# The memory norm of a fused two-block kernel: its sum of squares and its inverse root on other engines

## The reference, cut to what matters

```
def rmsnorm(x, g):
    xf = x.astype(jnp.float32)
    r = lax.rsqrt(jnp.mean(xf * xf, axis=-1, keepdims=True) + EPS)
    return (xf * r * g.astype(jnp.float32)).astype(x.dtype)

# in second_block, after the mixing part and the attention:
h = h + merged @ w_out[l]
c = rmsnorm(h, g_cross[l])
m = rmsnorm(mem, g_mem[l])            # mem: 256 positions x 1024
h = h + memory_cross_attention(c, m, w_q_cross[l], w_kv_cross[l], w_o_cross[l])
```

## Time and profile before

| | us |
|---|---|
| median of 3 runs | 2732.92 (2732.54 to 2734.36) |
| the profiled execution's own time | 2734.61 |
| its span, first to last instruction | 2732.6 |
| TensorE busy | 2679.1 (98%) |
| GpSimd busy | 1566.7 (57%) |
| VectorE busy | 1761.8 (64%) |
| ScalarE busy | 1120.9 (41%) |
| mean granted TensorE clock, of full speed | 0.995 |

### The profile page before, as it was taken

How to read it: one execution, slowest core, us unless ns; L and a number is a source line. 1 busy time by engine, 2 the same in 40 slices (tenths; PEclk the granted TensorE clock), 3 DMA queues, 4 the chain that set the end, 5 groups by cost and what they waited for, 6 DMA issues and landing times.

```text
span 2732.6 us, 37392 instructions
## 1 busy us (share of the span) xinstructions
PE 2679.1 (98%) x13692; PEld 2171.9 (79%) x13692; DVE 1761.8 (64%) x2628; ACT 1120.9 (41%) x2186; POOL 1566.7 (57%) x1175
## 2 busy tenths in 40 slices
PE   7999999999999999999999999999999999999998
PEld 6777788778888888878877777888788788888886
DVE  6776755587776777771133557763478777777776
ACT  5644422343444444454443335211354444444444
POOL 3233243567887778657722223456525787777884
PEclk9999999999999999999999999999999999999999
DMA  3110102111121221133211110342201211221112
GB/s 137 32 32 32 44 17 93 51 55 61 55 62 60 64 62 54 51 135 116 82 39 39 32 33 32 116 177 70 62 23 40 66 59 58 62 66 55 61 52 81
DMA packets 110702, 171.96 MB, mean 63 GB/s; under 512 B 7872, under 2 KB 61632, under 8 KB 108480
## 3 DMA queue, kind: packets, MB, share of 16 engines
q1 hardware_dynamic: 100352, 133.20, 15.4%
q10 hardware_dynamic: 10176, 36.44, 3.6%
HBM read 153.88 MB, written 15.73 MB: 62 GB/s over the span
## 4 chain that ended last, share of the span: by engine, by line
PE 90%; DVE 3%; POOL 3%; issue 2%; ACT 1%; DMA 1%; SPq 0%; ACTq 0%; DVEq 0%; POOLq 0%
PE PS L1485 13%; PE PS L1486 13%; PE PS L1487 13%; PE PS L1141 10%; PE PS L1143 9%; PE PS L1142 9%; PE PS L1757 2%; PE PS L1759 2%; PE PS L1758 2%; PE PS L1259 1%; PE PS L1177 1%; PE PS L1180 1%; PE PS L1178 1%; PE PS L1248 1%; PE PS L1630 1%
## 5 line engine op out<-in xcount | busy, mean ns | idle before, releaser
L907 POOL TENSOR_TENSOR WH<-WRAW,CST 128x512 fp32r<-128x512 f32 x164 | 185.4, 1131 | 709.4 <-PE PS L1143 618.3
L1141 PE MATMUL PS<-XH,WH 128*128 128x512 f32 x960 | 400.8, 418 | 2.6 <-POOL WL L909 1.7
L3374 DVE TENSOR_TENSOR H<-H,PS 128x512 f32<-128x512 f32 x560 | 367.4, 682 | 42.2 <-PE PS L1487 42.1
L1143 PE MATMUL PS<-XH,WL 128*128 128x512 f32 x960 | 377.2, 393 | 0.0
L1142 PE MATMUL PS<-XL,WH 128*128 128x512 f32 x960 | 376.5, 392 | 0.0
L942 POOL TENSOR_TENSOR WL<-WRAW,WH 128x512 fp32r<-128x512 f32 x174 | 252.3, 1451 | 118.4 <-ACT WH L2266 89.0
L942 POOL TENSOR_TENSOR WL<-XX,WH 128x512 fp32r<-128x512 f32 x148 | 202.1, 1367 | 91.4 <-ACT WH L2266 90.8
L1485 PE MATMUL PS<-XH,WH 128*128 128x512 f32 x640 | 249.4, 390 | 1.3 <-POOL WL L942 1.2
L1487 PE MATMUL PS<-XH,WL 128*128 128x512 f32 x640 | 249.0, 389 | 0.0
L1486 PE MATMUL PS<-XL,WH 128*128 128x512 f32 x640 | 249.0, 389 | 0.0
L1486 PE MATMUL PS<-PL,WH 128*128 128x512 f32 x624 | 242.8, 389 | 0.0
(11 more groups left out here) (443 smaller groups left out, 6104.8 us busy)
## 6 DMA issues: line engine op xcount, KB each, us to landing
WRAW<-ws SPq DMA_DIRECT2D x84, 512.0 KB, 3.5
WRAW<-ws SPq DMA_DIRECT2D x148, 256.0 KB, 2.6
XX<-ws SPq DMA_DIRECT2D x108, 256.0 KB, 2.7
RAWX<-ws SPq DMA_DIRECT2D x68, 256.0 KB, 2.6
gate_spill<-TG ACTq DMA_DIRECT2D x28, 256.0 KB, 2.1
H<-xT ACTq DMA_DIRECT2D x4, 1024.0 KB, 10.9
H<-xT ACTq DMA_DIRECT2D x2, 2048.0 KB, 10.9
h_spill<-H ACTq DMA_DIRECT2D x1, 4096.0 KB, 13.1
```

Of the source, the lines that this page charges most:

```text
L907: pool.tensor_tensor(WH[:, j, c], WRAW[:, j, c], ONES[:, 0:1].to_broadcast((P, 512)), ALU.mult).then_inc(hi_split, 1)
L1141: pe.matmul(out, WH[:, j, w], rh(kt), start=(n == 0), stop=False)
L1143: last = pe.matmul(out, WL[:, j, w], rh(kt), start=False, stop=(n == len(kts) - 1))
L3374: dve.tensor_tensor(x, x, PS[:, 4 + t], ALU.add).then_inc(h_added, 1)
```

## The change

The sum of squares is first folded on VectorE: three additions in XX, 128x1024, 128x512 and 128x256, halve the eight channel tiles to one. TensorE then makes one product of a 128x128 matrix of ones with that 128x256 tile, so the sum over channels arrives on every partition, and the 16 products and the two spreading products go. ScalarE divides by 1024, adds epsilon and writes 128x256 from PSUM to RAWX (Identity where the square root was). VectorE writes -0.5 into a column of STAT where the reciprocal was. GpSimd raises the 128x256 tile to that power into the other half of RAWX; for this, its loop over units is cut in two behind unit 63. VectorE's 8 multiplications read RAWX in SBUF where they read PSUM.

The diff, without the renamed semaphores:

```diff
--- before.py
+++ after.py
@@ -1110,7 +1110,13 @@
-            with pool.Fori(i + 1, U_FFN2 // 2) as i:
+            with pool.Fori(i + 1, U_WO2 // 2 + 2) as i:
+                for j in range(2):
+                    split_unit(i, j, True)
+            pool.wait_ge(mem_root, 1)
+            pool.wait_ge(mem_half, 1)
+            pool.tensor_tensor(RAWX[:, 1, 0:MEM], RAWX[:, 0, 0:MEM], STAT[:, 42:43].to_broadcast((P, MEM)), ALU.pow).then_inc(mem_inv, 1)
+            with pool.Fori(U_WO2 // 2 + 2, U_FFN2 // 2) as i:
                 for j in range(2):
                     split_unit(i, j, True)
             ffn(1, U_FFN2)
@@ -1842,18 +1848,9 @@
-                    pe.wait_ge(mem_sq, 1)
-                    for b in range(2):
-                        for kt in range(KT):
-                            last = pe.matmul(PS[:, MB, b:b + 1], XX[:, kt * MEM + b * P:kt * MEM + (b + 1) * P], ONES[:, 0:1],
-                                             start=(kt == 0), stop=(kt == KT - 1))
-                    last.then_inc(mem_sum, 1)
-                if n == 2:
-                    pe.wait_ge(mem_inv, 1)
-                    for b in range(2):
-                        last = pe.matmul(PS[:, MB, blk(b)], STAT[:, 42 + b:43 + b].to_broadcast((P, P)), IDENT,
-                                         start=True, stop=True)
-                    last.then_inc(mem_spread, 1)
+                    pe.wait_ge(mem_added, 3)
+                    pe.matmul(PS[:, MB, 0:MEM], ONES[:, 0:1].to_broadcast((P, P)), XX[:, 0:MEM], start=True,
+                              stop=True).then_inc(mem_sum, 1)
 
             pe.wait_ge(mem_split, 1)
@@ -2782,7 +2779,7 @@
                 if t == 1:
                     act.wait_ge(mem_sum, 1)
-                    act.activation(STAT[:, 40:42], PS[:, MB, 0:2], ACT.Sqrt, scale=1.0 / D, bias=v(V_EPS)).then_inc(mem_root, 1)
+                    act.activation(RAWX[:, 0, 0:MEM], PS[:, MB, 0:MEM], ACT.Identity, scale=1.0 / D, bias=v(V_EPS)).then_inc(mem_root, 1)
@@ -3646,14 +3643,20 @@
+                if t == 0:
+                    dve.wait_ge(mem_sq, 1)
+                    for n in range(3):
+                        w = 1024 >> n
+                        dve.tensor_tensor(XX[:, 0:w], XX[:, 0:w], XX[:, w:2 * w], ALU.add).then_inc(mem_added, 1)
+                        dve.wait_ge(mem_added, n + 1)
                 if t == 1:
                     dve.wait_ge(mem_root, 1)
-                    dve.reciprocal(STAT[:, 42:44], STAT[:, 40:42]).then_inc(mem_inv, 1)
+                    dve.memset(STAT[:, 42:43], -0.5).then_inc(mem_half, 1)
                 if t == 2:
-                    dve.wait_ge(mem_spread, 1)
+                    dve.wait_ge(mem_inv, 1)
                     for kt in range(KT):
                         last = dve.scalar_tensor_tensor(out=XX[:, kt * MEM:(kt + 1) * MEM], in0=MT[:, kt], scalar=v(V_GMEM + kt),
-                                                        in1=PS[:, MB, 0:MEM], op0=ALU.mult, op1=ALU.mult)
+                                                        in1=RAWX[:, 1, 0:MEM], op0=ALU.mult, op1=ALU.mult)
                     last.then_inc(mem_val, 1)
```

More of the change, by code:

```diff
@@ L517, in program @@
             "ya_val", "ya_high", "ya_split", "ys_val", "ys_high", "ys_split", "mix_read", "merged"))
-        mem_sq, mem_sum, mem_root, mem_inv, mem_spread, mem_val, mem_high, mem_split = map(sem, (
-            "mem_sq", "mem_sum", "mem_root", "mem_inv", "mem_spread", "mem_val", "mem_high", "mem_split"))
+        mem_sq, mem_added, mem_sum, mem_root, mem_inv, mem_half, mem_val, mem_high, mem_split = map(sem, (
+            "mem_sq", "mem_added", "mem_sum", "mem_root", "mem_inv", "mem_half", "mem_val", "mem_high", "mem_split"))
         vm_turned, vm_copied, final = map(sem, ("vm_turned", "vm_copied", "final"))
```

## The result

The changed kernel takes 2772.38 us (median of 4 runs, 2769.32 to 2777.93) against 2733.64 for the kernel before in the same comparison: ratio 1.0145, 95% interval 1.0133 to 1.0158. It is slower by 38.7 us, where 9.2 was forecast, and outside the range, which ended at 2760. Its profiled execution took 2769.32, with a span of 2767.4.

The account below looks back on a forecast made before the run. TensorE, busy 98% of the span, was taken to bound the kernel. Terms -4.1 (gain less folding delay) + 11.7 (wait) + 1.6 (low clock) = +9.2 us, on the median 2742.1; range 2730.5 to 2760.

Parts of the forecast that it names:

- What bounds, and the gain: TensorE, busy 98%, bounds; column sums (-3.47), low clock (-1.6) and spreading (-0.45) go, new product +0.45: -5.07 us.
- The folding: VectorE's first folding addition delays GpSimd's split of unit 62's second weight half, so TensorE stops 0.95 us inside unit 62.
- When the power starts: On GpSimd, behind unit 63's split and VectorE's memset of -0.5: the power starts at 1840.0.
- What the power costs: GpSimd's 128x256 power takes 6.8 us, scaled from VectorE's reciprocal; between 0.52 and 25.8 (forty passes).
- rival C: GpSimd's power takes 13 us or more; beyond 6.8 every microsecond counts in full; at 25.8, +28 us, 2761; chance 0.20.
- What waits for it: VectorE, held until the power ends, then taking turns with GpSimd's splits, makes TensorE wait 11.7 us ahead of unit 64.
- rival D: GpSimd's power doesn't hold VectorE, and multiplications on SBUF run as on PSUM; -2.6 us with power 6.8; chance 0.08.
- Low clock behind the wait: After TensorE's long pause ahead of unit 64, the low clock is charged once more, as after the column sums: +1.6 us.
- Edits at nothing: ScalarE's moved table load (1.28 us, covered by idle 2.16), memset, GpSimd's cut loop and later unit 66 weights cost nothing.

## Why the prediction was wrong

**What bounds, and the gain: right.** Sums, low clock and spreading left TensorE, -5.07 worked out. The folding cost 0.95 by the sum; the two products at the stop start 0.99 and 0.34 apart where they started 0.23 and 0.25 apart, 0.85 in all (the row's 0.60 counts only the idle time), and moving the folding gave back 0.85 of stage. Unit 64 could have started 1847.4 - 1824.2 = 23.2 us behind unit 62, 4.4 less than before; -4.1 was forecast.

**When the power starts: right.** 1840.0 was 10.7 us behind unit 62's start; it is 10.1 (1834.30 - 1824.19).

**What the power costs: this step failed.** The term for the power was mis-sized. "As the reciprocal is the nearest row in kind" gave 6.8, and forty passes 25.8 as the upper end; it is 41.14, six times the one and 1.6 times the other. The range, which ended at 2760, left out even the 2761 of that upper end. The scaling took VectorE's ratio of reciprocal to addition over to GpSimd, as if both did an iterated operation in the same way, and its split of a power into a logarithm, a product and an exponential stood on no row. The runs show a cost of 0.159 us for each element of a row, the same for 1 and for 128 partitions, for the exponents -0.5 and 1.0, in one instruction or two, where a whole multiplication of 128x256 takes 0.61 us, 0.002 an element of a row. No row read from the trace of the kernel before had anything near it, and the upper end should not have been drawn from a count of passes that I chose. The mechanism was rival C, given 0.20, with a price above its own example of 25.8. C's rule that every further microsecond counts in full would with 41.14 give 9.2 + 34.3 = +43.5; +40.1 came, for the reason below.

The Trainium skill (GPSIMD Engine Reference, Performance pitfalls for Q7 kernels) gives 4 cycles for each link of a dependent float32 chain. At the engine's 1.2 GHz (same page, Specifications) 41.14 us are some 190 cycles an element, which would be a chain of about 48 links. This is an estimate from the page; the runs show the total only.

**What waits for it: half right.** I had VectorE held for the power's whole length; this step failed too, though in the other direction and by less. Two additions of squares at 0.69, forty at 0.43 and the multiplications at 3.71 beside a power show that it is not held, but for perhaps 0.46 at its start. So rival D was right on this point and wrong on the multiplications: beside splits they take turns, 10.40. The steps as predicted would with 41.14 have given a wait of 11.7 + 34.3 = 46.0; 42.62 was measured. The difference is mostly two terms: VectorE's results and squares of unit 62 were done beside the power, so the multiplications started at its end and not 4.6 behind it (1846.8 to 1851.45), and they took 10.4 where 8.7 was worked out, eight turns and not six.

By the Trainium skill (SBUF — State Buffer, SBUF: two separate sides) a GpSimd instruction and a VectorE instruction with two SBUF inputs lock each other out: the one that starts first has the shared ports for its whole length. The splits agree here: 1.5 to 1.7 us for a 0.69 us addition. The power doesn't: beside its 41.14 us such an addition still takes 0.69, and the measurement decides.

**Low clock behind the wait: right in kind.** 1.6 was charged. Against the run with the multiplication, whose unit 64 keeps the full clock, it is 4.86 - 2.98 = 1.9; against the kernel before 1.7, because there TensorE also stops at unit 65's start for its weights (0.17 idle). The 1.6 was measured on other products, behind the column sums, so that it came this close is partly luck. **Edits at nothing: right.** With the change the table load stands at 1943.71, 1.28 long, and ScalarE still idles 0.86 behind it, so it is covered. In the run with the root in PSUM the load ahead of the norm's own root came onto the path, at the same 1.28.

In the prediction's terms the measured sum is -4.4 (unit 64 could start earlier) + 42.8 (TensorE's wait) + 1.7 (low clock) = +40.1, where -4.1 + 11.7 + 1.6 = +9.2 was forecast.

Settled by runs: the loss is the power's length (it goes with a multiplication in its place), and the length goes with the elements of a row. Open: why GpSimd needs so long for an element; no run looks inside the instruction, and none changes the values that are raised.

## What to carry to other kernels

An operation that no trace at hand shows has no upper bound from operations of another kind or engine; run it once, at two sizes, before it is put on a path. If GpSimd is to raise a value that is the same on all partitions, let it do so before the value is spread: 128x2 cost 0.71 us, 128x256 cost 41.14. Of the forms tried here the fastest took the norm's sum as one wide product with ones after a fold, left root and reciprocal in PSUM, so that what reads them doesn't take turns with GpSimd, and had the table loaded early and the norm's steps as early as they can be (0.9986 and 0.9987 of the time before). And measure past the end of the stage: in the run with the root in PSUM a wait of 2.50 us cost another 1.2 behind it, through the clock.

## What the runs showed of the hardware that I had not expected

- GpSimd's power of float32: 0.39 us and 0.159 us for each element of a row, from 2, 64, 128 and 256 elements (0.71, 10.52, 20.73, 41.13), whatever the number of partitions.
- Such a long instruction leaves VectorE alone, but for perhaps its start: 40 additions with two SBUF operands at 0.424 to 0.428 us beside it, one multiplication at its start at 0.93 in place of 0.48, while beside a 1.04 us multiplication or a 1.3 us subtraction such additions wait for its end.
- Sixteen one-column products over 3.47 us brought TensorE's clock down behind them (0.58 over the next 4 us); eight products of 256 columns over 3.45 us did not (1.00). A wait of 1.55 us did not bring it down either; behind the one of 2.50 us unit 64's products advanced by 0.12 at first and later by 0.21, with a mean granted clock of 0.63 over the unit.
